# Six value products of the memory attentions move between the router steps of the expert layers; heads' products alternate

## What is computed

```python
def expert_choice_ffn(h, w_router, w_gate, w_up, w_down):      # each trunk layer
    aff = softmax(einsum("bnd,de->bne", h, w_router))
    sel_w, sel_idx = lax.top_k(swapaxes(aff, 1, 2), cap)          # cap 32 of 256, 16 experts
    xs = h[sel_idx]
    y = (silu(xs @ w_gate) * (xs @ w_up)) @ w_down * sel_w
    return scatter_add(y, sel_idx)

def memory_cross_attention(x, mem, w_q, w_k, w_v, w_o):        # each layer of the second block
    q, k, v = x @ w_q, mem @ w_k, mem @ w_v                       # 4 heads of 256
    p = softmax(q k^T / 16)
    return (p v) @ w_o
```

## Time and profile before

| | us |
|---|---|
| runs (3), median | 3220.76 (3216.86 to 3226.86) |
| profiled execution, its own time | 3217.62 |
| its span | 3215.8 |
| TensorE busy | 2790.3 (87%) |
| VectorE busy | 857.6 (27%) |
| ScalarE busy | 343.2 (11%) |
| granted TensorE clock, mean share of full | 0.952 |

### The profile page before, as it was taken

One profiled execution on the slowest core, in us unless ns is written; L12 is line 12 of the kernel. 1 busy time (PEld: TensorE's weight loads), 2 busy tenths in 40 slices (PEclk: granted clock), 3 DMA queues, 4 the chain that ended last, 5 costly groups with the idle time before them and its releaser, 6 DMA issues.

```text
span 3215.8 us, 39515 instructions
## 1 busy us (share of the span) xinstructions
PE 2790.3 (87%) x16456; PEld 2008.8 (62%) x16456; DVE 857.6 (27%) x1758; ACT 343.2 (11%) x697; POOL 39.7 (1%) x70
## 2 busy tenths in 40 slices
PE   7999999978888879999555565699999999999998
PEld 3644454455655646888333233487888887888887
DVE  1322231242221234331211111389322102212200
ACT  0021120020000011220100000101210001111000
POOL 1000000000000001000000000000000000000000
PEclk9999999989999999999787878899999999999999
DMA  8434225149989973233599999743333443333441
GB/s 316 169 137 154 95 108 193 66 175 420 398 372 421 406 319 98 93 101 128 243 401 408 372 403 402 296 155 118 105 118 118 151 150 118 106 130 118 141 147 40
DMA packets 95644, 676.19 MB, mean 210 GB/s; under 512 B 11136, under 2 KB 12288, under 8 KB 15232
## 3 DMA queue, kind: packets, MB, share of 16 engines
q1 hardware_dynamic: 91488, 660.17, 52.4%
q0 software_dynamic: 4000, 13.64, 1.5%
HBM read 672.71 MB, written 1.05 MB: 210 GB/s over the span
## 4 chain that ended last, share of the span: by engine, by line
PE 74%; DMA 18%; DVE 3%; issue 2%; SPq 1%; ACT 1%; ACTq 0%; DVEq 0%
PE ps L566 28%; DMA ring<-units 18%; PE ps L827 10%; PE ps L947 10%; PE ps L852 2%; PE ps L1200 2%; PE ps L1005 2%; PE ps L1036 2%; PE ps L584 2%; PE ps L575 1%; PE ps L655 1%; PE ps L651 1%; PE ps L981 1%; SPq L474 1%; PE ps L776 1%
## 5 line engine op out<-in xcount | busy, mean ns | idle before, releaser
L947 PE MATMUL ps<-ring,arena 128*64 128x256 f32 (+1 forms) x6144 | 602.4, 441 | 259.7 <-DMA ring<-units 236.4
L947 PEld LDWEIGHTS ps<-ring,arena 128*64 128x64 f32 (+1 forms) x6144 | 374.6, 140 | 471.4 <-issue 346.0
L566 PE MATMUL ps<-h,ring 128*128 128x256 f32 (+1 forms) x2240 | 518.1, 393 | 4.9 <-ACT h L1359 4.9
L566 PEld LDWEIGHTS ps<-h,ring 128*128 128x128 f32 x2240 | 426.7, 191 | 94.0 <-issue 37.8
L827 PE MATMUL ps<-u,ring 128*128 128x512 f32 (+1 forms) x1024 | 339.5, 487 | 6.5 <-DMA ring<-units 6.5
L566 PE MATMUL ps<-arena,ring 128*128 128x256 f32 x1408 | 306.6, 379 | 4.7 <-DVE arena L2115 3.4
L566 PEld LDWEIGHTS ps<-arena,ring 128*128 128x128 f32 x1408 | 267.3, 190 | 42.1 <-DVE arena L2115 4.2
L827 PEld LDWEIGHTS ps<-u,ring 128*128 128x128 f32 x1024 | 193.6, 190 | 141.3 <-issue 119.6
L2011 DVE COPY u<-ps 32x512 f32<-32x512 f32 (+1 forms) x128 | 70.8, 553 | 310.7 <-PE ps L947 309.4
L2158 DVE SCALAR_TENSOR_TENSOR arena<-arena,vec 128x256 f32<-128x256 f32 x240 | 97.1, 481 | 0.0
L566 PE MATMUL ps<-u,ring 128*128 128x512 f32 (+1 forms) x256 | 87.8, 504 | 10.6 <-DVE u L1687 10.6
(11 more groups left out here) (313 smaller groups left out, 2446.6 us busy)
## 6 DMA issues: line engine op xcount, KB each, us to landing
ring<-units SPq DMA_DIRECT2D x624, 1024.0 KB, 10.1
arena<-quarters POOLq DMA_DIRECT2D x32, 256.0 KB, 2.9
h<-tokens SPq DMA_DIRECT2D x1, 2048.0 KB, 25.9
arena<-neighbours POOLq DMA_DIRECT2D x32, 64.0 KB, 3.9
arena<-tokens POOLq DMA_DIRECT2D x1, 2048.0 KB, 8.7
con<-constants SPq DMA_DIRECT2D x1, 1712.0 KB, 21.1
h<-memory POOLq DMA_DIRECT2D x1, 1024.0 KB, 6.0
out<-h SPq DMA_DIRECT2D x2, 512.0 KB, 3.2
```

Of the source, the lines that this page charges most:

```text
L566: last = nc.tensor.matmul(ps[:, g + j, 0:n], w[:, kt, j * P:(j + 1) * P], rhs[:, q * KT + kt, 0:n], start=(q == 0 and kt == 0), stop=(q == ...
L947: last = nc.tensor.matmul(ps[j * slots:(j + 1) * slots, bank, lo:lo + UC], lhsT[:, kt, 0:slots], w[j][:, kt, :], start=(kt == 0), stop=(kt ...
```

## The change

1. The last three of the four value units of each memory attention are put behind w_out of the trunk layer with the same number. A copy of the memory rows (`early_mem`) is loaded by POOL before each router. `early_values(lo, hi)` computes products lo to hi of the layer's 48 (16 per unit); calls of it stand between the router's steps. ScalarE copies a finished unit to `staged`, POOL stores it in DRAM, and loads all six back into `xv` in the second block, each layer's three behind the mixer. The memory attentions lose these units.
2. Router: affinities are transposed before `htok`; `pick` is made for the first four experts first; all four gathers come before the `wpick` transposes; ScalarE keeps gathers 1 and 3, VectorE 0 and 2; VectorE copies `wsel`; the squares (`sq1`) and other tiles lie elsewhere.
3. `mix` and the state space heads alternate between the two heads of a pair; `mix` waits once, for both copies.

```diff
@@ weight_stream
-        parts.append(units_of(i["w_out"][l]))
+        parts += [units_of(i["w_out"][l]), units_of(i["xa_w_v_2"][l])[1:]]
...
-        parts += early + [xa[l]["q"], xa[l]["v"][0 if l else 1:], xa[l]["o"]]
+        parts += early + [xa[l]["q"]] + ([xa[l]["v"][:1]] if l else []) + [xa[l]["o"]]
@@ gpsimd, per layer
+                pool.wait_ge(mixed, (24, 36)[l])
+                pool.dma_start(early_mem, ap["memory"]).then_inc(memory_loaded, 16)
+                for c in range(3):
+                    pool.wait_ge(values_staged, 3 * l + c + 1)
+                    pool.dma_start(ap["early_values"][l, c], staged[:, c, :, :]).then_inc(values_stored, 16)
...
+            pool.wait_ge(values_stored, 16 * 3 * DEPTH)
+            for l in range(DEPTH):
+                pool.wait_ge(go_ready if l else ssm_normed, KT)
+                for c in range(3):
+                    pool.dma_start(xv[:, :, (c + 1) * UC:(c + 2) * UC], ap["early_values"][l, c]).then_inc(values_back, 16)
@@ tensor, mix
-                    for j in range(2):
-                        pe.wait_ge(turned_kept, 2 * (before + i) + j + 1)
-                        for kb in range(first, 4):
+                    pe.wait_ge(turned_kept, 2 * (before + i) + 2)
+                    for kb in range(first, 4):
+                        for j in range(2):
@@ tensor, layer
+                def early_values(lo, hi):
+                    for n in range(lo, hi):
+                        c, b, kt = n // (TB * KT), n // KT % TB, n % KT
+                        if b == kt == 0:
+                            held["w"], held["c"] = unit(), c
+                            if c == 0:
+                                pe.wait_ge(memory_loaded, 16 * (l + 1))
+                        last = nc.tensor.matmul(ps[:, 3 if c == 1 else 7, b * S:(b + 1) * S],
+                                                early_mem[:, kt, b * P:(b + 1) * P], held["w"][:, kt, :],
+                                                start=(kt == 0), stop=(kt == KT - 1))
+                        if b == TB - 1 and kt == KT - 1:
+                            last.then_inc(units_used, 1)
...
-                project_and_normalize(merged[l], u, sq1, T, taken=False,
+                    early_values(0, 8 if l == 0 else 4)
+
+                project_and_normalize(merged[l], u, sq1, T, taken=False, between=shift_and_values,
                                       arrived=lambda kt: pe.wait_ge(merged_step, 16 * l + 13 + kt // 2))
...
+                early_values(8 if l == 0 else 4, 16 if l == 0 else 12)
@@ tensor, memory_attention
+                mixes = (mix_, own[0], own[0] + 1, own[1]) if l else (mix_, score, own[1], own[1] + 1)
...
-                values(pair())
+                if l:
+                    values(pair())
                 scores(3)
                 turn(0)
-                values(pair())
                 turn(1)
-                values(pair())
                 turn(2)
-                if l:
-                    values(pair())
-                turn(3)
                 drained()
-                for c in range(4):
-                    mix(c)
+                pe.wait_ge(values_back, 16 * 3 * (l + 1))
+                mix(0)
+                mix(1)
+                turn(3)
+                mix(2)
+                mix(3)
@@ tensor, state space
+                    for b in range(TB):
+                        for j in range(2):
+                            n = 2 * p + j
+                            last = nc.tensor.matmul(ps[j * HD:(j + 1) * HD, outs[2 + p % 2], b * P:S],
+                                                    xdt[:, b, n * HD:(n + 1) * HD],
+                                                    decay[p % 2][:, j, S * b:S + P * b],
+                                                    start=(b == 0), stop=(b == TB - 1))
@@ scalar, layer
+                def stage(c):
+                    act.wait_ge(units_used, at(units_used))
+                    A(staged[:, c, :, :], ps[:, 3 if c == 1 else 7, :].rearrange("p (b n) -> p b n", n=UC), ACT.Copy)\
+                        .then_inc(values_staged, 1)
@@ vector, layer
+                pick_experts(0, GROUP).then_inc(dve_to_pe, 1)
+                pick_experts(GROUP, E)
```

More of the change, by code:

```diff
@@ L328, in build @@
         pick = part(4096, 4, 640)
-        wpick = part(12288, 4, 512)
+        wpick = part(10752, 4, 512)
         logit = part(19712, 4, E)
@@ L2093, in memory_attention @@
                 softmax(2)
-                todo = list(range(0 if l else 1, 4))
-                keep_own_values(todo[0])
+                if l:
+                    keep_own_values(0)
                 softmax(3)
-                for c in todo[1:]:
-                    keep_own_values(c)
+                mixes = (mix_, own[0], own[0] + 1, own[1]) if l else (mix_, score, own[1], own[1] + 1)
                 for c in range(4):
                     dve.wait_ge(pe_to_dve, at(pe_to_dve))
-                    bank = (mix_, score, score + 1, turn_)[c]
+                    bank = mixes[c]
                     v.tensor_copy(xo[:, 2 * c:2 * c + 2, :], ps[:, bank, :].rearrange("p (a n) -> p a n", n=S))\
```

145 lines of the change are left out of this document (93 added, 52 removed).

## The result

Over four runs of each on one chip the changed kernel takes 3177.28 us (median; 3173.50 to 3184.05), the kernel before 3221.95. The ratio is 0.9864, with a 95% interval of 0.9841 to 0.9887: faster by 44.7 us. The prediction of 3174 us had -47 there.

What follows compares the result with a forecast made beforehand. TensorE, busy 87% of the span, bounds it except in DMA-bound expert stages and routers where it waits for other engines. -32 + 0 - 14 - 0.5, about -47 from 3217.6, gives 3170.6, as median 3174; range 3168 to 3181.

Steps and rivals of the forecast that it cites:

- Memory attentions: Both memory attentions lose three value units, 20.7 us per layer, less bared waits and clock: -32 us in sum.
- The bared wait: Layer 0's memory attention, from the end of the scores to the first copy: 3.5 us exposed net; in layer 1 2.6.
- a term of 1: Layer 1's memory attention: 1 us charged for clock lost behind idle time; 2 us charged in layer 0.
- rival E: Memory attentions gain nothing, as removed products only bared a wait for values from DRAM or the softmax: 3206; chance 0.03.
- Routers: 41.4 us of value products go between the router's steps: layer 0 -4 us, layer 1 +4.5, together 0.
- the value product "at 0.43 us": Routers: each value product placed between the steps was counted at 0.43 us.
- L947 at 680.7 against 683.11: Layer 0: the experts' first row, L947, starts at 680.7 instead of 683.11.
- end where they did: Layer 0's router: the logits begin at 649.7 warm, interleaved with four value products, and end at the same time as before.
- Rival B: Fillers delay more than worked out, 3 us more per layer at four places, 12 together: 3186; chance 0.15.
- Heads: Alternating heads in L776 saves 0.55 us per full step, 24 of them, and 0.1 for 12 half steps: -14 us.
- State space: State space heads, eight pairs of 0.8 us, with VectorE busy 5.44 of 5.50 us a round: -0.5 us, at most -3.

Runs made afterwards that it cites:

- run 4: Changed kernel with the logits' four alternating value products put together behind the eighth round; 3178.70 us, ratio 0.9875.
- run 5: Changed kernel with a value product behind each of the logits' eight rounds instead of the first four; 3185.23 us in a single execution.
- run 6: Changed kernel with two early value units per layer instead of three, the third back in the memory attention between transposes; 3171.54 us, ratio 0.9856.
- Run 1: Kernel before with only the heads' products alternating and the same reordering in the state space; 3209.06 us against 3218.38, ratio 0.9969.
- run 8: Changed kernel unaltered, run again as a control beside the kernel before; 3177.81 us, ratio 0.9878.

## Why the prediction was right, and where it was off

The forecast was 3174 us; 3177.28 was measured, within its own range of 3168 to 3181. Step by step:

**Memory attentions: right.** -32.3 was predicted in two terms (15.2 and 17.1), -31.7 came. The bared wait, estimated at 3.5 us net in layer 0, is 3.24; the clock cost 1.5 instead of 2. In layer 1 the waits are 2.18 and 0.78, less 0.34 that was there before, 2.6 as estimated. The 2.0 us given back there, for a term of 1, are 1.7 of clock in the norm and 0.35 of wait; in the second execution the clock cost 2.9, in the attention. That the sum came so close in the first is partly luck. Nothing waits for the values loaded back, so rival E is out.

**Routers: the mechanism was right, two sizes were off.** Forecast 0 (-4 and +4.5), measured +4.2. The mis-sized step is the value product "at 0.43 us" in the logits: alone it is, but between products of another form a round costs 0.30 more. Four rounds make 1.2 us per layer (run 4, and run 5 in the other direction). I had L947 at 680.7 against 683.11, 2.4 us earlier; it came 0.5 earlier from the sums. In layer 1 it came 6.4 later for 4.5. So 1.9 us are missing in each. In layer 0 the places came as worked out up to the logits (14.9 us behind the sums for 14.8), and from there to the affinities it was 9.8 us for 7.5; all that follows is late by this. The sentence that failed is that the interleaved logits "end where they did". For that they had 4.7 us, from 649.7 to 654.4. They took 6.6: 1.7 for the four products, 3.7 for the eight rounds at full clock (0.46 each), 1.2 for the changes. So by 0.7 us they would not have fitted without the changes either. Taking the alternation away does not win the time back (run 4), since the norm's tiles then pace the rounds. In layer 1 it does, 1.2 of the 1.9. The other 0.7 lies in the same stretch: from the first logits to the affinities it took 9.7 us where my places leave 8.0, and from there to the experts all is as forecast. Rival B, 12 us of delay spread over the fillers, had the right sign and three times the size.

**What stood in the sum and had no price of its own:** the order alone gains 7.5 us in layer 0, and the two blocks of eight products behind the ranks and the gathers cost 4.7 there and 5.6 in layer 1 up to the experts' start (run 6). My working said that the values are late behind `pick` and had the gathers and the experts start behind the two blocks, but it never asked what they cost. The numbers came out, because both were in the path that I followed. The better kernel could have been read from it: two fillers that are each waited for and hide little.

**Heads: right, mis-sized.** 0.48 us per full step for 0.55, 0 per half step for 0.1: -11.6 for -14. I gave L793 0.9 us and it takes 1.03. That the 1.51 us of before were "serial" was misread: in its trace the second head's first product starts 0.49 us behind the first head's, which still has three of its eight to start. Alternating brings the two starts within 0.01 us. The Trainium skill ("TensorE: Matmul & The Clock Gate", Part 3) lets a weight load overlap a running product only when the row group differs. Both heads use all rows, and the trace has 16 instructions in 1.03 us against 1.51; so here the measurement speaks against that rule. Run 1 shows that the gain is the heads' own.

**State space: right in size, for another reason.** -0.2 came for -0.5, and a round still takes 5.51 us. My reason was that VectorE is busy throughout. But TensorE is too (5.50 of 5.50 us in the earlier trace rows), and the two heads' products themselves are no shorter, 0.81 us to the next step before and 0.80 after. Timelines of TensorE, before (L1180, L1182) and after (L1231):

```profile
2229.30 0.66 PE L1180 MATMUL ps<-u,arena 128*64 128x256 f32 x4
2229.78 0.39 PE L1182 MATMUL ps<-u,arena 128*64 128x128 f32 x4
```

```profile
2229.33 0.87 PE L1231 MATMUL ps<-u,arena 128*64 128x256 f32 x8
```

Each L1180 row holds the products of both heads, though the program has one head's L1182 between them. So the heads, four instructions each, ran side by side before the change too, and the new order had nothing to add. The same holds for the half steps of the attentions.

**Not in the sum:** clock that is lost elsewhere. 2.2 of the +2.9 in layer 0's attention, 1.5 in layer 1's logits with the heads alone. I took the clock as fixed in all places that the change doesn't touch, and it was not; it isn't even fixed for one kernel (run 8).

## What to carry to other kernels

Fillers pay where TensorE would idle, up to the length of that wait and, where they save its clock, beyond; placed where the partner is already done they cost most of their length (2.3 to 3.0 of 3.46 us in run 6). So count them per wait, not per stage, and give the surplus back to the place that it came from: here two of three units hid in the routers, all but 2.3 and 0.4 us of 13.8 per layer, and most of the third in the attention's own gap. In a filler's place, don't change between forms of weights at every instruction; here the same work in blocks was a quarter shorter. And check an earlier start at the end of the stage behind it: here 4.7 us won at the start of layer 0's experts were gone at their end.

## What was not expected of the hardware

A change between products with 32 and with 128 columns of weights cost 0.15 us, 0.30 per round, in both directions of the test (1.18 us per round against 0.45 + 0.43).

The granted clock behind a wait of the same length differs from one version to the next, and from one execution of the same kernel to the next. Behind waits of 2.6 to 3.4 us the same 128 instructions took 7.11, 8.80 or 9.96 us (mean granted clock 1.00, 0.83 and 0.70 around them). In the two executions of the changed kernel the row behind 3.4 us took 8.80 and 7.11, and the norm's squares behind the same 1.86 us took 5.41 and 3.72. So 2 to 3 us can come and go at one place with no edit at all; what decides it was not settled here.

Two heads in the two column halves already ran side by side with four instructions each, one head after the other in program order. With eight each they overlapped only in part, and alternating made 1.03 us of 1.51.
